# Decoder layer on one core: the first two experts' tokens gathered in one pass, PSUM banks released by the additions, cross-attention's queries in steps of two pieces, one rounded weight and one expert load moved

## The reference

```python
def reference(x, mem, ...):                       # x: 256 tokens x 1024
    h = x
    h = h + ssd_mixer(rms_norm(h, mixer_norm), ...)           # Mamba-2 mixer
    h = h + memory_cross_attention(rms_norm(h, xattn_norm), rms_norm(mem, mem_norm), w_q, w_kv, w_o)
    h = h + moe_ffn(rms_norm(h, ffn_norm), ...)               # 32 experts, 4 per token
    return rms_norm(h, final_norm)

def memory_cross_attention(h, mem_n, w_q, w_kv, w_o):         # 4 heads of 256
    q = (h @ w_q).reshape(...)
    k, v = halves of mem_n @ w_kv
    p = softmax(q k^T / 16)
    return (p v) @ w_o

def moe_ffn(h, w_router, b_router, w_gate_up, b_gate_up, w_down, b_down):
    gates, experts = softmax of the 4 largest of (h @ w_router + b_router)
    for each chosen expert e:
        gate = min(x @ w_gate[e] + b, 7);  up = clip(x @ w_up[e] + b, -7, 7)
        out += g * (((up + 1) * gate * sigmoid(1.702 * gate)) @ w_down[e] + b_down[e])
```

## Time and profile before

| | |
|---|---|
| median of 3 runs | 1278.32 us (1276.92 to 1278.54) |
| profiled execution: its time | 1277.69 us |
| profiled execution: its span | 1275.9 us |
| PE busy | 1183.7 us (93%) |
| DVE busy | 394.6 us (31%) |
| ACT busy | 265.8 us (21%) |
| moved | 454.28 MB, mean 356 GB/s |
| TensorE granted clock | mean 0.99 of full speed |

### The profile page before, as it was taken

One profiled execution on the slowest core, in us unless ns is written; L12 is line 12 of the kernel. 1 busy time (PEld: TensorE's weight loads), 2 busy tenths in 40 slices (PEclk: granted clock), 3 DMA queues, 4 the chain that ended last, 5 costly groups with the idle time before them and its releaser, 6 DMA issues.

```text
span 1275.9 us, 15455 instructions
## 1 busy us (share of the span) xinstructions
PE 1183.7 (93%) x6205; PEld 626.1 (49%) x6205; DVE 394.6 (31%) x713; ACT 265.8 (21%) x414; POOL 7.5 (1%) x27
## 2 busy tenths in 40 slices
PE   7999999989999999999988889899999989999986
PEld 6998887888634344333333333334433333343422
DVE  5887666546311122111111111212111111121112
ACT  6555445445211111010110001101101010010102
POOL 1000000000000000000000000000000000000000
PEclk9999999999999999999999999989999999999998
DMA  9454323476789999999999999999999999999994
GB/s 314 170 199 140 125 92 122 167 281 260 305 359 428 428 428 428 428 429 429 428 427 429 428 429 428 429 427 427 428 430 429 427 429 425 393 428 430 429 427 182
DMA packets 55078, 454.28 MB, mean 356 GB/s; under 512 B 6332, under 2 KB 6500, under 8 KB 30468
## 3 DMA queue, kind: packets, MB, share of 16 engines
q1 hardware_dynamic: 54864, 453.74, 85.8%
q10 hardware_dynamic: 180, 0.07, 0.0%
HBM read 452.74 MB, written 1.05 MB: 356 GB/s over the span
## 4 chain that ended last, share of the span: by engine, by line
PE 56%; DMA 39%; DVE 2%; issue 1%; ACT 1%; DVEq 0%; SPq 0%; ACTq 0%
DMA ring<-in_moe_w_down 39%; PE ps L880 14%; PE ps L909 12%; PE ps L549 3%; PE ps L551 3%; PE ps L550 3%; PE ps L853 2%; PE ps L564 2%; PE ps L919 2%; PE ps L565 2%; PE ps L566 2%; PE ps L683 1%; PE ps L537 1%; PE ps L891 1%; PE ps L837 1%
## 5 line engine op out<-in xcount | busy, mean ns | idle before, releaser
L909 PE MATMUL ps<-ring,wring 128*64 128x512 f32 x1024 | 232.1, 600 | 53.7 <-DMA ring<-in_moe_w_down 52.3
L880 PE MATMUL ps<-ring,wring 128*64 128x512 f32 x1024 | 225.0, 597 | 0.0
L909 PEld LDWEIGHTS ps<-ring,wring 128*64 128x64 f32 x1024 | 70.4, 137 | 203.0 <-issue 124.1
L997 ACT ACTIVATE wring<-ps 128x512 f32<-128x512 f32 (+1 forms) x105 | 53.0, 521 | 532.3 <-PE ps L880 438.7
L1682 DVE COPY wring<-ps 128x512 f32<-128x512 f32 x32 | 22.1, 691 | 410.7 <-PE ps L880 410.7
L880 PEld LDWEIGHTS ps<-ring,wring 128*64 128x64 f32 x1024 | 72.4, 138 | 141.1 <-issue 141.0
L1690 DVE TENSOR_TENSOR wring<-ps,bguT 128x512 f32<-128x512 f32 x64 | 44.0, 687 | 309.1 <-PE ps L891 309.1
L880 PE MATMUL ps<-mid,wring 128*64 128x512 f32 x512 | 116.6, 609 | 3.6 <-DVE wring L1696 2.4
L997 ACT ACTIVATE ysb<-ps 128x512 f32<-128x512 f32 x36 | 21.5, 598 | 271.3 <-PE ps L909 265.7
L880 PEld LDWEIGHTS ps<-mid,wring 128*64 128x64 f32 x512 | 37.2, 140 | 72.7 <-issue 72.4
L853 PEld LDWEIGHTS ps<-wring 128*128 128x128 f32 x480 | 55.8, 191 | 23.5 <-issue 23.5
(11 more groups left out here) (306 smaller groups left out, 1389.0 us busy)
## 6 DMA issues: line engine op xcount, KB each, us to landing
ring<-in_moe_w_gate_up SPq DMA_DIRECT2D x64, 2048.0 KB, 22.9
ring<-in_moe_w_down SPq DMA_DIRECT2D x64, 2048.0 KB, 25.5
mid<-in_moe_w_gate_up SPq DMA_DIRECT2D x32, 2048.0 KB, 23.3
wring<-in_moe_w_gate_up SPq DMA_DIRECT2D x16, 2048.0 KB, 26.2
hs<-in_moe_w_gate_up SPq DMA_DIRECT2D x16, 2048.0 KB, 27.7
wring<-in_ssd_w_in SPq DMA_DIRECT2D x10, 2048.0 KB, 8.0
wring<-in_xa_w_kv SPq DMA_DIRECT2D x4, 2048.0 KB, 8.5
wring<-in_ssd_w_out SPq DMA_DIRECT2D x4, 2048.0 KB, 7.7
```

The costliest lines, as they stand in the source:

```text
L880: last = mm(ps[a][SLOTS * half:SLOTS * (half + 1), :], xs[:, m, c % 2, :], w[:, kk, c0:c0 + 512], start=s + kk == 0, stop=s + kk == GP)
L909: last = mm(ps[D_BANK][SLOTS * half:SLOTS * (half + 1), :], act[:, k, :], w[:, kk, 512 * half:512 * (half + 1)], start=k == 0, stop=k == K ...
L997: return nc.scalar.activation(out_, in_, func, **kw)
```

## The change

Six edits. (1) `KV_BANK[6]` is bank 3 in place of bank 0; the transposes of `xn2` go to banks 4 to 7, which are free once the additions to `h` are done (`h_ok` 4), and the queries to banks 0 to 3; `kv_out(6)` moves behind the copies of `xq`. (2) `W_Q`'s second half is split (`w_hi`, `w_lo`) ahead of the `xq` copies on both engines, and the queries start with two pieces of `xq` at a time. (3) The additions of attention's output go by column half instead of token half, and the copies `hT_out` and the norm's parts are put in another order around them. (4) The rounded half of `W_O + 1` lies in weight slot 1 (`wlo` 2 and 3) instead of `lo_ring`; this leaves expert 0's second down slot free once the queries are done, and SP starts its load at `q_ps` 4 instead of behind the output weights. The experts' small tiles trade places in `wring` to make room. (5) One operation makes the selection for experts 0 and 1, one `first_gather()` of 128 columns gathers both ahead of `gate_up(0, 0)`. (6) In `swiglu`, for every expert, `gate_b` and `up_b` are given by the two additions themselves; both limits come behind them, and the sigmoid waits for a new semaphore `lim_ok` behind the gate's limit.

```diff
--- before.py
+++ after.py
-        xr = part(wring, 6144, 8192, r="p (k s) -> p k s", k=KD)
+        xr = part(wring, 2048, 4096, r="p (k s) -> p k s", k=KD)
...
-        onehot = part(wring, 1536, 1792, r="p (t j s) -> p t j s", t=TC, j=2)
+        onehot = part(wring, 5632, 5888, r="p (t j s) -> p t j s", t=TC, j=2)
...
-        xn = part(wring, 4096, 6144, r="p (t n) -> p t n", t=TC)
+        xn = part(wring, 0, 2048, r="p (t n) -> p t n", t=TC)
...
-        KV_BANK = (0, 1, 0, 1, 0, 1, 0, 7)
+        KV_BANK = (0, 1, 0, 1, 0, 1, 3, 7)
...
-                 2 * late_)
+                 late_ + (late_[0], ((wlo, 2), (wlo, 3))))
...
                 if n == W_O + 1:
+                    sp.wait_ge(q_ps, 4)
+                    load_down(sp, 0, 1)
                     sp.wait_ge(sc_ps, XH)
                     load_gate_up(sp, 0, 0, 1)
...
-            for s in range(DP):
-                sp.wait_ge(wo_ps, 8 + 2 * s)
-                load_down(sp, 0, s)
+            sp.wait_ge(wo_ps, 8)
+            load_down(sp, 0, 0)
+            sp.wait_ge(wo_ps, 10)
             load_gate_up(sp, 1, 1, 1)
             load_gate_up(sp, 1, 1, 2)
-            sp.wait_ge(hot_first, 1)
+            sp.wait_ge(hot_ok, 1)
...
-            pe.wait_ge(kv_sb, 7)
-            norm_transposes(2, xn2)
+            pe.wait_ge(h_ok, 4)
+            norm_transposes(2, xn2, 4)
...
-            for half in range(2):
-                pe.wait_ge(nt_dve, 8 + 2 * half + 2)
+            for j in range(4):
+                pe.wait_ge(nt_dve, 8 + j + 1)
                 for b in range(2):
-                    queries(b, 0, range(4 * half, 4 * half + 4))
+                    queries(b, 0, range(2 * j, 2 * j + 2))
             for b in range(2):
                 queries(b, 1, range(KD)).then_inc(q_ps, 1)
-            split_T(W_Q + 1, (6, 7), xq, q_ps, lambda b: None)
+            split_T(W_Q + 1, (2, 3), xq, q_ps, lambda b: pe.wait_ge(kv_sb, 7) if b else None)
...
-                    pe.wait_ge(h_ok, 4 + 2 * t + half + 1)
+                    pe.wait_ge(h_ok, 4 + 2 * half + t + 1)
...
-            def first_gather(j):
+            def first_gather():
 
                 for half in range(2):
-                    bank = ps[G_BANK if j else (D_BANK, G_BANK)[half]]
                     for m in range(4):
                         k = 4 * (m // 2) + 2 * half + m % 2
-                        c0 = SLOTS * (4 * half * j + m)
                         for t in range(TC):
-                            last = mm(bank[:, c0:c0 + SLOTS], xn[:, t, P * k:P * (k + 1)], onehot[:, t, j, :],
-                                      start=t == 0, stop=t == TC - 1)
-                    if j == 0:
-                        last.then_inc(first_ps, 1)
-                if j:
-                    last.then_inc(gath_b, 1)
+                            last = mm(ps[(D_BANK, G_BANK)[half]][:, P * m:P * (m + 1)], xn[:, t, P * k:P * (k + 1)],
+                                      onehot[:, t, :, :], start=t == 0, stop=t == TC - 1)
+                    last.then_inc((first_ps, gath_b)[half], 1)
...
-            pe.wait_ge(hot_first, 1)
+            pe.wait_ge(hot_ok, 1)
             pe.wait_ge(normed, 2 * 3 + TC)
-            first_gather(0)
+            first_gather()
             gate_up(0, 0)
-            pe.wait_ge(hot_ok, 1)
-            first_gather(1)
             transposes(0, 0)
...
             w_hi(W_Q, 0)
-            kv_out(6)
+            w_hi(W_Q, 1)
             for b in range(4):
                 act_.wait_ge(nt_ps, 8 + b + 1)
                 for k in (2 * b, 2 * b + 1):
-                    last = fn(xq[0][:, k, :], ps[b][:, SEQ * (k % 2):SEQ * (k % 2 + 1)], ACT.Copy,
+                    last = fn(xq[0][:, k, :], ps[4 + b][:, SEQ * (k % 2):SEQ * (k % 2 + 1)], ACT.Copy,
                               scale=parT[:, g_xa + k:g_xa + k + 1])
                 last.then_inc(nt_act, 1)
-            w_hi(W_Q, 1)
+            kv_out(6)
...
+            def first_out(half):
+
+                act_.wait_ge((first_ps, gath_b)[half], 1)
+                fn(xs[:, 4 * half:4 * half + 4, :, :].rearrange("p m j c -> p (m j c)"), ps[2 + half][:, :],
+                   ACT.Copy).then_inc((xsa_ok, xsb_ok)[half], 1)
...
-                act_.wait_ge(gate_b, 2 * i + (c + 1))
+                act_.wait_ge(lim_ok, 2 * i + (c + 1))
...
             act_.wait_ge(h_ok, 6)
+            fn(xn[:, 1, 0:512], h[:, 1, 0:512], ACT.Square, accum_out=nrm[:, 5, 0:1])
+            act_.drain()
+            fn(nrm[:, 5, 1:2], nrm[:, 5, 0:1], ACT.Identity, bias=eps[:, 0:1], scale=1.0 / D)
+            act_.wait_ge(h_ok, 7)
             fn(xn[:, 0, :], h[:, 0, :], ACT.Square, accum_out=nrm[:, 3, 0:1])
             act_.drain()
             fn(nrm[:, 3, 0:1], nrm[:, 3, 0:1], ACT.Sqrt, bias=eps[:, 0:1], scale=1.0 / D).then_inc(std, 1)
             hT_out(0)
-            act_.wait_ge(h_ok, 7)
-            fn(xn[:, 1, 0:512], h[:, 1, 0:512], ACT.Square, accum_out=nrm[:, 5, 0:1])
-            act_.drain()
-            fn(nrm[:, 5, 1:2], nrm[:, 5, 0:1], ACT.Identity, bias=eps[:, 0:1], scale=1.0 / D)
-            hT_out(1)
             act_.wait_ge(h_ok, 8)
             fn(xn[:, 1, 512:1024], h[:, 1, 512:1024], ACT.Square, accum_out=nrm[:, 3, 1:2])
             act_.drain()
             fn(nrm[:, 3, 1:2], nrm[:, 3, 1:2], ACT.Sqrt, bias=nrm[:, 5, 1:2], scale=1.0 / D).then_inc(std, 1)
+            hT_out(1)
...
             w_lo(W_Q, 0)
+            w_lo(W_Q, 1)
             for b in range(4):
                 dve.wait_ge(nt_act, 8 + b + 1)
                 for k in (2 * b, 2 * b + 1):
                     last = v.scalar_tensor_tensor(out=xq[1][:, k, :], scalar=parT[:, g_xa + k:g_xa + k + 1],
-                                                  in0=ps[b][:, SEQ * (k % 2):SEQ * (k % 2 + 1)],
+                                                  in0=ps[4 + b][:, SEQ * (k % 2):SEQ * (k % 2 + 1)],
                                                   in1=xq[0][:, k, :].bitcast(F32), op0=ALU.mult, op1=ALU.subtract)
                 last.then_inc(nt_dve, 1)
-            w_lo(W_Q, 1)
...
-            for t in range(TC):
-                add_out(7, t, 2)
-                if t == 1:
-                    hT_out(1)
-                norm_chunk(3, t, xn, h, g_ffn)
-                if t == 0:
-                    hT_out(0)
+            def add_part(n, t):
+                dve.wait_ge(wo_ps, 7 + 2 * n + t)
+                r = h[:, t, 512 * n:512 * (n + 1)]
+                v.tensor_tensor(r, r, ps[4 + 2 * n + t][:, :], ALU.add).then_inc(h_ok, 1)
+
+            add_part(0, 0)
+            add_part(0, 1)
+            add_part(1, 0)
+            norm_chunk(3, 0, xn, h, g_ffn)
+            add_part(1, 1)
+            hT_out(0)
+            hT_out(1)
+            norm_chunk(3, 1, xn, h, g_ffn)
...
-                                    b4[:, a, :, :].unsqueeze(3).to_broadcast([P, 4, 2, SLOTS]), ALU.add)
-                    if a == 0:
-                        dve.drain()
-                        v.tensor_scalar(gu[:, 0, :, :, :], gu[:, 0, :, :, :], LIMIT, None, ALU.min).then_inc(gate_b, 1)
+                                    b4[:, a, :, :].unsqueeze(3).to_broadcast([P, 4, 2, SLOTS]),
+                                    ALU.add).then_inc((gate_b, up_b)[a], 1)
                 dve.drain()
-                v.tensor_scalar(gu[:, 1, :, :, :], gu[:, 1, :, :, :], LIMIT, -LIMIT, ALU.min, ALU.max).then_inc(up_b, 1)
+                v.tensor_scalar(gu[:, 0, :, :, :], gu[:, 0, :, :, :], LIMIT, None, ALU.min).then_inc(lim_ok, 1)
+                v.tensor_scalar(gu[:, 1, :, :, :], gu[:, 1, :, :, :], LIMIT, -LIMIT, ALU.min, ALU.max)
...
-            one_hot(0, 0).then_inc(hot_first, 1)
+            v.tensor_tensor(onehot[:, :, :, :], iota[:, 0:SLOTS].unsqueeze(1).unsqueeze(1).to_broadcast([P, TC, 2, SLOTS]),
+                            rank[:, :, 0:2].unsqueeze(3).to_broadcast([P, TC, 2, SLOTS]),
+                            ALU.is_equal).then_inc(hot_ok, 1)
             v.tensor_tensor(gate[:, :, :], gate[:, :, :], gsum[:, :, 0].unsqueeze(2).to_broadcast([P, TC, NE]),
                             ALU.mult).then_inc(gate_ok, 1)
-            one_hot(1, 1).then_inc(hot_ok, 1)
```

44 lines of the change are left out of this document (16 added, 28 removed).

## The result

The changed kernel took 1268.02 us (median of 6, 1265.86 to 1268.72); before ran beside it in 1277.62 (1272.52 to 1278.75): a ratio of 0.9929 [0.9914, 0.9943]. The forecast was 1271.6 and its range ended at 1268.6, just above this: 9.6 us between the two medians, where the sum had 6.4. The profiled execution took 1268.72 with a span of 1266.9, against 1277.69 and 1275.9: 9.0 us less.

What follows compares the result with a forecast made beforehand. The end was taken as the moment the weight stream is full for good, plus the bytes left. Stream 6.2 us earlier plus 0.2 in the last expert made 6.4 us, giving 1271.6 us, range 1268.6 to 1274.0.

Steps and rivals of the forecast that it cites:

- the first gather's: Gather ahead of expert 0: one 128-column gather costs 0.3 us more than the 5.31 of 64 columns; `gate_up(0, 0)` starts 2.8 earlier.
- Rival 2: Clock recovers sooner at the first gather, or does not fall: gain 9.8 us, 1268.2; half of it 1270; chance 0.24.
- Queries, "1.9 earlier": Transposes and query products: no wait for `mid`, no 1.60 us pause, so the second half begins at 267.7 instead of 269.63.
- Rival 1: Clock falls ahead of the queries, in a pause grown to 2.5 us: price 1.8 us, 1273.4; chance 0.14.
- The rule weighed: Ahead of the queries: transposes don't count as busy, so queries begin at half clock, 1.8 us; the profile row showed full clock.
- Router, 3.1 in all: Reordered additions and copies around the transposes of `h`: router's product at 333.7 instead of 336.80, 3.1 us earlier in all.
- Second gather gone, 2.9: Behind `gate_up(0, 0)`: the second gather's 3.71 us goes, 0.8 of waiting takes its place, 2.9 us gained.
- `swiglu`, 1.3: Ahead of expert 1: banks free when the second addition ends, TensorE at 370.75 instead of 372.04, 1.3 us gained.
- The stream, "2.8 + 3.4": Weight stream reaches expert 3 by 2.8 + 3.4 = 6.2 us earlier, a little less than TensorE's 7.0, full from expert 2 on.
- The moved down piece: Expert 0's second down piece, loaded earlier in a stream gap (290 to 295 us): costs nothing and gains nothing.
- Edit 6, 0.2: `swiglu` in the last expert, in the open: one wait less between passes, between 0 and 0.6 us, taken as 0.2.

Runs made afterwards that it cites:

- batch 3: A set of follow-up runs measured on one chip beside the kernel before, which took 1277.05 us there (1272.56 to 1279.47, 23 executions).
- narrow_both: Changed kernel, both experts still gathered ahead, but each 128-column product split into two of 64 columns; 1277.42 us (1271.85 to 1278.92), ratio 0.9999.
- before_again: The kernel before, unchanged, timed and profiled again; 1276.2 us (1273.1 to 1279.06, 12 executions), the profiled execution 1273.80.
- gather_apart: Changed kernel with edit 5 undone: two gathers of 64 columns, each at its old place; 1270.61 us (1267.42 to 1273.02), ratio 0.9955.
- limits_first: Changed kernel with edit 6 undone: limits ahead of the release of the banks in all experts; 1269.66 us (1268.07 to 1269.83), ratio 0.9949.
- fill_pause: Changed kernel plus two unread products of 512 columns in TensorE's pause ahead of the queries; 1267.58 us (1266.01 to 1269.13), ratio 0.9931.
- old_queries: Changed kernel with edits 1 and 2 undone: banks, order of splits and query steps as before; 1269.27 us (1268.88 to 1271.59), ratio 0.9949.
- only_gather: Kernel before with edit 5 alone, one selection and one 128-column gather; 1273.02 us (1271.99 to 1276.88, 12 executions), ratio 0.9982.
- late_down: Changed kernel with expert 0's second down piece loaded behind the output weights again; 1270.68 us (1269.68 to 1271.83), ratio 0.9953.
- slow_look_b: One profiled execution of the changed kernel with both experts gathered ahead in 64-column products; span 1276.6 us, gather 11.89 us.
- narrow_again: Second measurement of the changed kernel with both experts gathered ahead in 64-column products; 1273.32 us (1270.06 to 1279.15), ratio 0.9985.

## Why the prediction missed

**The step that failed** is the first gather's: "The gather of 64 columns took 5.31 us ahead of expert 0, at a clock of 0.59", to which I added 0.3 for the width, and the same for the pass behind it, 15.64 taken over unchanged. From the last piece of expert 1 to the first of expert 2 (SP's queue) this made 354.59 - 343.88 + 0.3 = 11.0 us; it was 349.13 - 341.64 = 7.49. That is 3.5 us too much. Of the profiled 9.0 against 6.4 this is more than the whole: 3.5, less 1.6 that the queries gave less, and 0.65 by which this execution reached the end of the mixer sooner (260.28 - 259.63), make 2.6. I took one execution's clock for a property of the place, where before itself needs 350.86 - 343.42 = 7.44 in another. Rival 2 named this way and its time, 1268.2, at 0.24, so that 1268.0 was met by a rival's number, not by the forecast's. It was also right on the condition ("come back earlier or not fall"), but not on its reason: nothing here shows more work for each weight load as the cause, only the width as what differs.

**What the gain is made of.** Before's executions are not of one sort: of its 23 times in batch 3, 15 lie at 1276.5 and above, 8 at 1276.1 and below. Its fall at the gather is seen in the one profile of 1277.69 and in none of the three of 1272.88 to 1274.86; that the upper half of its times has it is argued from this and from the clusters of narrow_both, not shown. (before_again's twelve times split the same way, six at 1273.1 to 1275.1 and six at 1277.3 to 1279.1.) Between profiles with equal clocks at queries and gather, before_again and after, the gain is 1272.0 - 1266.9 = 5.1, and this is the change's order. The other 3.9 of the profiled 9.0 (1275.9 - 1272.0) are the fall in the first profile of before, which none of the eight profiled gathers of 128 columns had. That the width keeps it off is likely, not shown.

**Queries, "1.9 earlier".** From the end of the mixer's products to the transposes of `h` before took 332.69 - 260.28 = 72.4, whether the clock fell (before_again 72.4) or not: the pause of 1.60 hid the fall. With the change it is 70.2 and 70.4 where it stays up (gather_apart, 329.71 - 259.49; limits_first, 330.11 - 259.69) and 72.1 where it falls (after, 331.71 - 259.63). So the 1.9 were right at full clock (2.0 to 2.2), and are 0.3 with the fall, which six of the eleven profiles with the new order have (fill_pause aside), and three of the six with the old. Rival 1 came true as a mechanism, at its price of 1.8, and hid in a larger gain elsewhere.

**The rule weighed.** The row of 1.00 at 260 to 265 spoke against the page. It could not tell: it is 1.00 in before_again too, and the fall is in the stretch behind it. At 265 to 270 the first profile has 1.00. Three more profiles of before, with the same pauses of 0.69 and 1.97 around the transposes, have 0.66 there. Two more kernels keep that order with the same pauses, old_queries and only_gather, and both have 1.00 (in this order):

```profile
265.00:270.00 5.00, 3.41 (x29) 3.24 (x29) 4.24 (x5) 5.00 (x4) 0.00 (x0) 1.00 0.99 423
```

```profile
265.00:270.00 5.00, 3.41 (x29) 3.24 (x28) 4.23 (x5) 5.00 (x3) 0.00 (x0) 1.00 1.00 426
```

That transposes don't count as busy for the clock (the Trainium skill, TensorE: Matmul & The Clock Gate, Part 4: PE-mode transpose) is thus compatible with three of six profiles of this stretch, and by itself doesn't say what the other three did. The same page (Part 1, What's actually happening) says that how many products run slow at the start of one kernel varies from run to run. Ahead of the first gather of kernel before the traces vary in the same sense, 5.31 against 3.79 us.

**Router, 3.1 in all, so 1.2 of its own.** 11.21 - 9.95 = 1.26. Right, and undoing the edit gives it back.

**Second gather gone, 2.9, and `swiglu`, 1.3.** Between the first two passes 7.19 - 3.19 = 4.0 instead of 4.2. Right; the chain shows the VectorE copy (0.70) that takes its place, as the prediction had it. But the stream hides most of it: with the second gather, gather_apart asks for expert 3 only 0.4 us behind the moment at which the stream would be free.

**The stream, "2.8 + 3.4".** The second term was exact: 377.61 - 354.59 - 19.6 = 3.4. The first measured 5.46 instead of 2.8, for the reasons above and because of the 0.65. 5.5 + 3.4 = 8.9 of the 9.0. That it can't follow TensorE's 9.44 was right too.

**The moved down piece, "Its gain is nothing too".** Wrong, by 2.2 between medians. The prediction said that one more piece would "just have fitted", but by its own numbers it ends at 347.5 + 4.9 = 352.4, 0.6 behind the 351.8 at which it had expert 2 asked for; in late_down that moment is 347.55, and the stream is through at 349.9. A margin of less than nothing hung on a time that came 2.7 earlier in after (349.13).

**Edit 6, 0.2.** At expert 1 the clock also stayed up more often with it, by the column above. Against limits_first the medians differ by 1.2 (1269.66 and 1268.48), across two batches, and no run separates the 0.2.

## What to carry to other kernels

Before costing a stretch in which TensorE ran at half clock, take several profiles: a fall that is in some executions and not in others is a probability, and a small edit can change it. Where each loss is handed to a stream, write the end as the latest of the moments that can fill it; one such line, its constant taken from one profile, gave 13 of 16 others here within some 0.5 us, and it tells at once which later saving is free. Where a stretch is split into many small products, wide ones are worth a trial: here 16 of 128 columns took 3.84 us, and the same work in 32 of 64 took 7.36 at full clock and 11.8 to 12.3 in three of five profiles.

## What the runs showed of the hardware

- TensorE at 0.50 (1.2 GHz) while it was busy 5.00 of 5.00 us, with 64-column float32 products (slow_look_b, 345 to 350). It came back only in the 512-column products behind them. None of the eight profiled 128-column gathers did this. Why the width matters stays open: no run separates the columns of a product from the number of products or of weight loads (narrow_both doubles both).
- The same program (narrow_both, narrow_again) had its times in two clusters, 1270.1 to 1274.0 and 1277.1 to 1279.2, on each of two chips. A mean granted clock of 0.987 to 0.990 goes with the upper one, 0.989 to 0.993 with the lower.
- A gather of 128 columns costs 3.84 us, one of 64 columns 3.79, both for 32 recorded products at full clock: half the columns saved 0.05.
